# Gathering expert rows in 1 KB quarters and transposing them on VectorE instead of TensorE

## The reference, cut to what matters

```python
idx, gates = route(xf, w_router, router_bias)      # 8 of 64 experts for each of 640 tokens
# rows sorted by expert: 640 * 8 = 5120 (token, expert) pairs
hb = jax.nn.silu(xb @ w_gate[e]) * (xb @ w_up[e])  # 1024 -> 256, twice
rows = hb @ w_down[e]                              # 256 -> 1024
routed = segment_sum(rows * row_gate, row_tok)     # back to tokens, plus one shared expert
```

## Time and profile before

| | us |
|---|---|
| median of 3 runs | 1044.88 |
| lowest, highest | 1041.33, 1049.09 |
| span of the profiled execution | 1047.0 |
| TensorE busy in it | 1005.6 (96%) |
| expert loop, first gate/up to last wait for weights | 402.3 to 934.2 |

### The profile page before, as it was taken

The page is one execution under the profiler, slowest core; times in us unless marked ns, Lnnn a source line. Parts: engine busy times, 40 slices in busy tenths (PEclk is TensorE's granted clock), DMA queues, the critical chain, the costliest instruction groups (busy, mean ns, idle before and its releaser), DMA issues.

```text
span 1047.0 us, 17787 instructions
## 1 busy us (share of the span) xinstructions
PE 1005.6 (96%) x7124; PEld 453.0 (43%) x7124; DVE 333.5 (32%) x839; ACT 227.0 (22%) x537; POOL 161.6 (15%) x233
## 2 busy tenths in 40 slices
PE   6999999999999999999999999999999999989996
PEld 2655555565455553443333333333333333423342
DVE  0122224766126773321211111112111111112388
ACT  1121103766122330111211111112111111112111
POOL 1000001300122022111222112212221121111000
PEclk9999999999999999999999999999999999989998
DMA  9955417600101189999999999999999999997896
GB/s 373 406 213 210 155 57 167 255 2 2 46 35 41 47 352 392 382 411 422 422 421 419 419 421 417 415 419 415 417 412 413 414 394 399 420 372 300 345 409 255
DMA packets 59676, 321.64 MB, mean 307 GB/s; under 512 B 9748, under 2 KB 10396, under 8 KB 31560
## 3 DMA queue, kind: packets, MB, share of 16 engines
q1 hardware_dynamic: 43184, 272.71, 64.7%
q0 software_dynamic: 14240, 43.34, 10.5%
q10 hardware_dynamic: 2168, 4.43, 1.1%
HBM read 298.78 MB, written 31.39 MB: 315 GB/s over the span
## 4 chain that ended last, share of the span: by engine, by line
PE 81%; DMA 8%; DVE 7%; ACT 2%; issue 1%; SPq 0%; POOL 0%; DVEq 0%; ACTq 0%
PE bank L2120 30%; PE bank L2140 14%; PE bank L1711 8%; PE bank L1882 5%; DMA ring<-in_w_up 5%; PE bank L2092 4%; PE bank L1976 3%; PE bank L1738 2%; PE bank L1909 2%; PE bank L1700 2%; DMA ring<-expert_rows 2%; PE bank L1989 2%; PE bank L1895 1%; PE bank L1982 1%; DMA ring<-in_w_mod 1%
## 5 line engine op out<-in xcount | busy, mean ns | idle before, releaser
L2120 PE MATMUL bank<-ring,reg_h 128*32 128x512 f32 x2448 | 334.2, 595 | 6.7 <-DMA ring<-in_w_up 4.9
L2120 PEld LDWEIGHTS bank<-ring,reg_h 128*32 128x32 f32 x2448 | 99.2, 110 | 191.4 <-issue 191.2
L2140 PE MATMUL bank<-ring,reg_y 128*32 128x512 f32 x1224 | 170.5, 594 | 2.8 <-ACT reg_y L1075 1.9
L2120 PE MATMUL bank<-reg_p,reg_h 128*32 128x512 f32 x688 | 143.8, 602 | 0.0
L1538 DVE TENSOR_TENSOR reg_h<-reg_p,bank 128x256 f32<-128x256 f32 x49 | 20.7, 422 | 320.3 <-ACT reg_p L1093 286.3
L1093 ACT ACTIVATE reg_p<-bank 128x256 f32<-128x256 f32 x49 | 18.8, 383 | 310.4 <-PE bank L2120 310.4
L1711 PE MATMUL bank<-ring,reg_h 128*128 128x384 f32 (+2 forms) x256 | 84.3, 488 | 0.0
L769 POOL DMA_INDIRECT expert_rows<-reg_y,rowc x47 | 47.2, 1004 | 239.5 <-DVE reg_y L1523 229.2
L2140 PEld LDWEIGHTS bank<-ring,reg_y 128*32 128x32 f32 x1224 | 46.4, 110 | 83.7 <-issue 78.9
L1523 DVE TENSOR_SCALAR reg_y<-bank,reg_p 128x512 f32<-128x512 f32 x49 | 36.8, 751 | 129.2 <-PE bank L2140 129.0
L2140 PE MATMUL bank<-reg_p,reg_y 128*32 128x512 f32 x344 | 72.3, 593 | 0.0
(11 more groups left out here) (279 smaller groups left out, 968.6 us busy)
## 6 DMA issues: line engine op xcount, KB each, us to landing
ring<-in_w_gate SPq DMA_DIRECT2D x51, 1024.0 KB
ring<-in_w_up SPq DMA_DIRECT2D x51, 1024.0 KB
ring<-in_w_down SPq DMA_DIRECT2D x51, 1024.0 KB
ring<-in_w_mod SPq DMA_DIRECT2D x21, 1024.0 KB, 8.1
ring<-expert_rows SPq DMA_DIRECT2D x19, 1024.0 KB, 14.7
reg_p<-in_w_gate SPq DMA_DIRECT2D x13, 1024.0 KB
reg_p<-in_w_up SPq DMA_DIRECT2D x13, 1024.0 KB
reg_p<-in_w_down SPq DMA_DIRECT2D x13, 1024.0 KB
```

The costliest lines, as they stand in the source:

```text
L2120: last = pe.matmul(bank[2 + p][R * j:R * j + R, :], xg_t[:, p, k * P + R * j:k * P + R * j + R], w_gu(homes[n % SLOTS])[:, k], start=(k == ...
L2140: last = pe.matmul(bank[y_banks(b)[hf]][R * j:R * j + R, :], h_t[:, p, i * P + R * j:i * P + R * j + R], w_dn(homes[n % SLOTS])[:, i, 512 ...
```

## The change

- **h2 in DRAM** is stored with its values permuted, so that one row is four quarters of 256 values (1 KB) and, within a quarter, the eight values that belong to one contraction step come from eight runs of 32. POOL makes this copy (`quarters_first`) into one buffer `h2perm`, and SP stores it instead of ACT. The gates go to a tensor of their own.
- **The gather** of a block becomes five indirect DMAs: four of 128 rows of 1 KB and one of 128 rows of 256 B. Place 32g + r of gather j takes quarter g of row r of tile j; its index is 4 x token + g, made once for all blocks by 32 small matmuls and two DVE instructions (`quarter_at`). The copies of index columns on POOL go; columns of the tables are used directly.
- **The x transposes on TensorE** and the two half copies go. One DVE `transpose` of 32x32 pieces over 128x1024 writes `xg_t`.
- **The h transpose** becomes eight matmuls against the identity, each on 32 columns of the array, in two alternating halves of bank 4, issued in the middle of the next block's gate/up.
- **The order** on TensorE is one block at a time: gate/up of b with the h of b-1 inside, then down of b-1. POOL: gather of b+4, then scatter of b. DVE: `gated(b)`, `x_in(b+2)`, `y_out(b-1)`.

```diff
-            def gather(p):
-                pool.indirect_dma_start(out=xg[:, p, :], out_offset=None, in_=h2_dram,
-                                        in_offset=bass.IndirectOffsetOnAxis(ap=tokc[:, p:p + 1], axis=0),
+            def gather(p, quarters, tokens):
+
+                for j in range(4):
+                    pool.indirect_dma_start(out=xq[:, p, 2 * P * j:2 * P * (j + 1)], out_offset=None, in_=h2_quarters,
+                                            in_offset=bass.IndirectOffsetOnAxis(ap=quarters(j), axis=0),
+                                            bounds_check=4 * NTOK - 1, oob_is_err=False).then_inc(s_xg[p], 16)
+                pool.indirect_dma_start(out=xgate[:, p, :], out_offset=None, in_=gates_dram,
+                                        in_offset=bass.IndirectOffsetOnAxis(ap=tokens, axis=0),
                                         bounds_check=NTOK - 1, oob_is_err=False).then_inc(s_xg[p], 16)
...
+            def quarters_first(t):
+                pool.wait_ge(s_h2, t + 1)
+                at_least(pool, s_h2o, 16 * t)
+                pool.tensor_copy(h2perm.rearrange("p (g k i) -> p g k i", g=4, k=KD),
+                                 h2row[:, t % 2, :].rearrange("p (g i k) -> p g k i", g=4, k=KD)).then_inc(s_h2p, 1)
...
+            for b in range(KEPT):
                 next_gather(b + 4)
-                next_gather(b + 5)
+                next_scatter(b)
...
-            sp.wait_ge(s_xg[0], 16)
+            sp.wait_ge(s_xg[0], 80)
             load_gate_up(4, e[4])
...
-            def xt_half(b, p, source=bank[1]):
-                dve.wait_ge(s_xt, b + 1)
-                dve.tensor_copy(xg_t[:, p, 512:1024], source[:, :]).then_inc(s_xb, 1)
...
+            def x_in(b):
+                p = b % 2
+                dve.wait_ge(s_xg[p], 80 * (b // 2 + 1))
+                at_least(dve, s_g, b - 1)
+                dve.transpose(xg_t[:, p, :], xq[:, p, :]).then_inc(s_xb, 1)
...
-            def block_transposes(b, p, gathered, banks=(0, 1)):
-                pe.wait_ge(s_xg[p], gathered)
-                v = xg[:, p, 0:D].rearrange("p (q k) -> p k q", k=KD)
-                for k in range(KD):
-                    last = pe.transpose(bank[banks[k // 4]][:, (k % 4) * P:(k % 4 + 1) * P], v[:, k, :], ident)
-                last.then_inc(s_xt, 1)
...
+            def block_h(b):
+
+                pe.wait_ge(s_h, b + 1)
+                at_least(pe, s_he, b)
+                v = hh[:, b % 2, :].rearrange("p (c r j) -> p j c r", j=2, r=R)
+                for j in range(2):
+                    for c in range(4):
+                        o = 2 * P * (b % 2) + j * P
+                        last = pe.matmul(bank[4][R * c:R * c + R, o:o + P], v[:, j, c, :], ident, start=True, stop=True)
+                last.then_inc(s_ht, 1)
...
+            pe.wait_ge(s_tokf, 1)
+            for j in range(4):
+                o = 2 * NT + NQ * j
+                for g in range(4):
+                    last = pe.matmul(bank[6][R * g:R * g + R, o:o + NQ], ident[:, R * j:R * j + R], tok_f[:, 0:NQ],
+                                     start=True, stop=True)
+            last.then_inc(s_rep, 1)
...
+            for b in range(2, KEPT):
+                block_gate_up(b, lambda: block_h(b - 1))
                 block_down(b - 1)
```

More of the change, by code:

```diff
@@ L392, in build @@
         s_h2 = sem("h2_rows_ready")
-        s_h2o = [sem(f"h2_rows_out{i}") for i in range(2)]
+        s_h2p = sem("h2_rows_in_quarters")
+        s_h2o = sem("h2_rows_out")
         s_t2 = sem("h2_transposed")
@@ L628, in _ @@
                 broadcast(g2bc[:, cond, :], mod_dram[5, cond:cond + 1, :], s_g2)
+            for t in range(T):
+                sp.wait_ge(s_h2p, t + 1)
+                sp.dma_start(h2_dram[t * P:(t + 1) * P, :], h2perm).then_inc(s_h2o, 16)
             sp.wait_ge(s_op, 2 * T)
@@ L759, in scatter @@
[L759 to L769, removed]
+            pool.wait_ge(s_tab, 2)
@@ L770, in scatter, with next_gather @@
+            def next_gather(b):
+                if b < NQ:
+                    if b >= 2:
+                        pool.wait_ge(s_xb, b - 1)
+                        pool.wait_ge(s_gc, b - 1)
+                    gather(b % 2, lambda j: quarter_at[:, j, b:b + 1], tok_i[:, b:b + 1])
+            def scatter(p, rows):
+                pool.indirect_dma_start(out=y_dram, out_offset=bass.IndirectOffsetOnAxis(ap=rows, axis=0),
                                         in_=yb[:, p, :], in_offset=None,
@@ L789, in next_scatter @@
-            def next_scatter(b):
[L790 to L794, removed]
+            def next_scatter(b):
+                pool.wait_ge(s_ya, b + 1)
+                pool.wait_ge(s_yb, b + 1)
+                scatter(b % 2, row_i[:, b:b + 1])
+            for b in range(3):
+                next_gather(b)
             pool.wait_ge(s_sht, T)
             pool.memset(zeros, 0.0).then_inc(s_idx, 1)
+            pool.wait_ge(s_idx, 1)
@@ L797, in _ @@
             for b in (KEPT, KEPT + 1):
[L798 to L802, removed]
+                pool.indirect_dma_start(out=y_dram, out_offset=bass.IndirectOffsetOnAxis(ap=row_i[:, b:b + 1], axis=0),
                                         in_=zeros, in_offset=None,
@@ L1526, in _ @@
             shared_sum(1)
-            def x_in(b):
-                xt_half(b, b % 2, bank[xt_banks(b)[1]])
-                block_gates(b, b % 2, ecol[:, b:b + 1], gate_s[:, b:b + 1])
             x_in(0)
@@ L2142, in block_down @@
                 last.then_inc(s_y, 1)
+            pe.wait_ge(s_tokf, 1)
[5 more added lines that the diff above has]
+            last.then_inc(s_rep, 1)
+            for j in range(4):
+                o = 4 * NQ + XBLK * (j + 1)
+                for g in range(4):
+                    last = pe.matmul(bank[7][R * g:R * g + R, o:o + XBLK], ident[:, R * j:R * j + R], tok_f[:, NQ:NT],
+                                     start=True, stop=True)
+            last.then_inc(s_rt, 1)
             shared_down(0)
```

269 lines of the change are left out of this document (99 added, 170 removed).

## The result

The kernel after takes 1063.2 us (median of 4 runs, 1061.1 to 1064.1); its ratio to the kernel before is 1.0174, with a 95% interval of 1.0143 to 1.0204. It is slower, by 1.4 to 2.0%. A fourth run of before took 1953.5 us and is left out as a slow one. The profiled execution has a span of 1060.8 us where that of before had 1047.0: +13.8. By the medians the loss is 18.3 us (1063.2 against 1044.9). The traces can't say where the other 4.5 us lie: the profiled execution of before was the slowest of its three (1049.1), that of after is 0.6 us under its median (1062.6).

What follows compares the result with a forecast made beforehand. The prediction took full DMA engines to bound the expert loop. Packets +16, unevenness +3, start +4 and end -4 made +19 on 1047.0, so 1066, less 2.1 for the profiled span: 1064 us, range 1036 to 1098.

Steps and rivals of the forecast that it cites:

- The limit: Expert loop: DMA engines 99.8% full for 565 us, TensorE at the same pace; a faster TensorE would wait.
- Packets, +16: Gathers in the expert loop: each quarter row its own packet, 210 ns against 170 per row, plus tiny packets; +16 us.
- Unevenness, +3: Expert loop: gather and weight queues take turns by packet, 54 turns against 18 per block; +3 us over the loop.
- Start, +4: First gate/up and weight stream: index table and a later fifth gather DMA delay them, +4 us (2 to 8).
- TensorE: Expert loop: a block takes 10.75 us against 11.6; the 0.85 us are worth nothing before the last awaited load.
- VectorE and GpSimd: Expert loop: DVE transpose 1.3 us, up to 2.5, and POOL's indirect DMAs 1.44 us apart, both hidden beside other work.
- End, -4: After the last awaited load: TensorE's remaining gate/up and downs get shorter, -4 us (-6 to -2).
- Rival 1: Gathers: quarters cost no more than whole rows, being joined or overlapped; 1045 us, chance 0.25.
- Rival 2: Expert loop: turns between queues starve the gathers, TensorE stops often and drops to half clock; 1099 us, chance 0.2.
- Rival 3: Expert loop: TensorE is the limit, so its 0.85 us per block are gained; 1007 us, chance 0.1.

Runs made afterwards that it cites:

- the last of the kernels with whole rows: The kernel after with one gather of whole rows instead of four of quarters, and without TensorE's overflow loop and its branch: 1043.8 us, ratio 0.998.

## Why the prediction was right, and where not

The forecast was 1064.0 with +19 in the sum; measured are 1063.2 and, between the two profiled executions, +13.8. The direction and the limit were right; the reason given, more packets for the gathers on full DMA engines, accounts for 3.4 of the stream's 10.6 us. That the median came within 1 us is luck: the terms of +16, +3, +4 and -4 stand against +10.6, 0, +1.2 and +2.0, errors of both signs, and the executions that were profiled lie 4.5 us nearer to each other than the medians.

- **The limit.** Right: DMA sets the pace until the last awaited weights. The earlier trace rows read as full meant full: 36 us less for TensorE gave 0 in the kernel before, 44 MB less to load gave 60 us in the kernel after. One reading of mine was too large: of the 10 MB that the engines move in 25.19 us some 8 are weights (189.37 of 231.52 MB), so under three homes were queued, and not more than three.
- **Packets, +16.** The step that failed is the row price: I took a quarter row as a packet of its own, 4 x 48 + 18 against 170. The Trainium skill ("DMA: Bandwidth & Descriptors", Queues, rings and completion order) was nearer with its packets of typically 9 to 17 descriptors. The counts agree in that rows are joined, 144 packets per block for 640 places, but not in the number: four rows of 1 KB to a packet, eight of 256 B, one of 4 KB. The work of q0 in the loop is 0.187 x 577 = 107.9 us per engine in place of 0.185 x 565 = 104.5: +3.4, for smaller packets and more completions. What I had no term for is the weight queue: 0.811 x 577 = 467.9 us in place of 0.813 x 565 = 459.3, for nearly the same bytes. That is 2.464 us per MB in place of 2.426; for 189.9 MB, +7.3. Together 10.7, near the 10.6 of the stream; the shares are given to 0.1%, which is 0.6 us in each of these. The sign and the place were right, the size by half too large, and most of it comes from packets that the change doesn't touch. What makes those dearer stays open.
- **Unevenness, +3.** None: the share stays at 99.8%. With joined packets a gather and scatter have about 23 turns per block and not 54.
- **Start, +4.** It was +1.2. (The range for it is 2 to 8 in its own paragraph of the prediction and 4 to 10 in the last; 1.2 lies under both.)
- **TensorE.** 10.75 us per block forecast, 10.74 measured; the eight h matmuls 0.44 (0.45). Waits of 1.4 us per block forecast; they are 39.4 / 45 = 0.9, and not spread but in nine stops of up to 7.9 us, all but the shortest (1.3 us) with matmuls at the lower clock after them. Since DMA is the limit, that clock costs nothing until the end.
- **VectorE and GpSimd.** The transpose takes 1.24 us (1.3), and GpSimd issues a gather every 1.3 us (1.44):

```profile
L1500 DVE STREAM_TRANSPOSE reg_h<-reg_h 128x1024 f32<-128x1024 f32 x38 | 47.1, 1239 | 1.6 <-DMA reg_h<-gate_rows,tok_i 1.6
```

```profile
L769 POOL DMA_INDIRECT reg_h<-h_rows,reg_p x149 | 150.1, 1008 | 47.3 <-issue 47.3
```

- **End, -4.** It was +2.0. Up to the end of the last down of the loop the gain is there: 27.7 us (945.97 to 973.66) in place of 32.0 (934.22 to 966.25). I had no term for the branch behind it: it takes 7.3 us in place of 1.8, the lower clock some more, and the sums on TensorE, which begin at 1007.15, become the path to the end. Without the branch and with whole rows the end is 108.5 us, -4.3 to before. A cost that no line of the diff names, where the skipped code lies in TensorE's program, was worth 6 to 7 us (6.7 with quarters, 87.1 against 80.4, and 6.7 with whole rows).
- **Rival 1**, quarters joined, had the mechanism right and the time wrong: 1045 would have needed what the last of the kernels with whole rows shows, no dearer weight packets and no stop behind a branch; that one takes 1043.8.
- **Rival 2**, starved gathers, did not come: VectorE's transpose waited 1.6 us in all for gathers, 450 to 900 us. Before with five gathers went past its time, 1099, but with slow downs, not with late rows.
- **Rival 3**, TensorE as the limit, is refuted by the kernel before with less work for TensorE (ratio 0.9992) and the kernel after with less to load (0.9595).

## What to carry to other kernels

When the DMA engines are full, count what a change does to their packets and to the price of everybody else's packets; work taken from the compute engines comes back as waits. To see which engine is the limit, take work from one at a time: one kernel with fewer transposes and one with fewer bytes said it. And look behind skipped loops: beside full queues TensorE stopped there for 3.4 to 4.5 us with each block of code that was fetched, and 16 or 40 instructions more made one stop out of two.

## What the runs showed of the hardware that I had not expected

- Rows of an indirect DMA are joined into packets: 128 rows of 1 KB in 32, of 256 B in 16; rows of 4 KB and more stay alone (18160, 15808 and 14240 packets on q0).
- The price of an 8 KB packet on one queue depends on the form of another queue's gather: 2.42 us per MB and engine beside rows of 4 KB over 128 partitions, 2.46 beside quarters, 2.82 beside gathers of the same 32 rows into 32 partitions at a time.
- Behind a taken branch TensorE stopped for 3.5 us (one fetch) or 7.3 us (two) in the same kernel, depending on where its instructions lie, and for 1.8 us without a fetch in the kernel before. An increment of a semaphore on TensorE takes about 0.15 us (256 of them held the first matmul until 40.15 us; 16 made a stop 2.4 us longer).
- The same matmuls can fall out of step for most of a program (downs of 4.6 to 6.3 us in place of 3.45) after changes that touch none of them. This is open.
